# Folding the first block's closing norm into the next block's first norm, in a two-block network on one core

## The reference, cut to what matters

```
def rmsnorm(x, w): ...            # x / sqrt(mean(x*x) + 1e-6) * w

def first_block(x, ...):
    x = x + lru_mlstm_layer(rmsnorm(x, e_norm[0]), ...)
    x = x + ssd_layer(rmsnorm(x, o_norm[0]), ...)
    return rmsnorm(x, final_norm)

def second_block(x, norm1_g, w_in, ...):
    for l in range(2):
        h = rms_norm(x, norm1_g[l])
        q, k, v, gu, gv = jnp.split(h @ w_in[l], ...)
        ...
        x = x + mixed @ w_o[l]
        x = x + conv_gated_ffn(rms_norm(x, norm2_g[l]), ...)
    return x
```

## Time and profile before

| | |
|---|---|
| median of three runs | 3615.18 us |
| profiled execution | 3617.5 us |
| its span, first to last instruction | 3615.7 us |
| PE busy | 3509.0 us (97%) |
| DVE busy | 2717.7 us (75%) |
| ACT busy | 1893.6 us (52%) |
| POOL busy | 1648.0 us (46%) |
| mean granted PE clock | 0.989 |
| HBM read | 618.75 MB, 172 GB/s over the span |

### The profile page before, as it was taken

The page is one execution under the profiler, slowest core; times in us unless marked ns, Lnnn a source line. Parts: engine busy times, 40 slices in busy tenths (PEclk is TensorE's granted clock), DMA queues, the critical chain, the costliest instruction groups (busy, mean ns, idle before and its releaser), DMA issues.

```text
span 3615.7 us, 53014 instructions
## 1 busy us (share of the span) xinstructions
PE 3509.0 (97%) x19644; PEld 3020.8 (84%) x19644; DVE 2717.7 (75%) x4031; ACT 1893.6 (52%) x2865; POOL 1648.0 (46%) x1435
## 2 busy tenths in 40 slices
PE   8998999999999999998999999999998999999999
PEld 7887888888888788777888888888886888888888
DVE  8768886689899954676788758877676788758875
ACT  6555785455555544765444434444765444434443
POOL 4325672167787700143366405653143366306640
PEclk9999999999999999998999999999998999999999
DMA  5544556655555556433555665556543555665566
GB/s 193 169 152 137 167 180 187 188 181 180 165 169 176 167 162 182 151 128 111 181 187 187 184 189 187 187 181 192 177 133 109 185 187 187 186 189 187 187 184 178
DMA packets 177041, 624.38 MB, mean 173 GB/s; under 512 B 19784, under 2 KB 25616, under 8 KB 175760
## 3 DMA queue, kind: packets, MB, share of 16 engines
q1 hardware_dynamic: 171216, 606.11, 53.6%
q10 hardware_dynamic: 5568, 14.89, 1.1%
HBM read 618.75 MB, written 2.17 MB: 172 GB/s over the span
## 4 chain that ended last, share of the span: by engine, by line
PE 71%; DVE 10%; POOL 5%; ACT 3%; issue 3%; ACTq 0%; POOLq 0%; DVEq 0%
PE psG L517 42%; PE psG L515 23%; DVE WL L1274 3%; PE psG L514 2%; PE psM L540 1%; POOL SQ L1724 1%; ACT WH L763 1%; ACT L783 1%; DVE sdx L1287 1%; POOL SQ L1743 1%; POOL sdx L1726 1%; DVE Et L1527 1%; DVE Et L1534 0%; POOL GV L1864 0%; DVE Y L1279 0%
## 5 line engine op out<-in xcount | busy, mean ns | idle before, releaser
L517 PE MATMUL psG<-H,WH 128*128 128x512 f32 x5655 | 2028.4, 399 | 0.0
L1274 DVE TENSOR_TENSOR WL<-RAW,WH 128x1024 fp32r<-128x1024 f32 (+1 forms) x1162 | 1488.7, 1281 | 578.9 <-ACT WH L763 577.1
L763 ACT ACTIVATE WH<-RAW 128x1024 fp32r<-128x1024 f32 (+1 forms) x1162 | 1214.6, 1045 | 970.0 <-PE psG L517 956.3
L515 PE MATMUL psG<-H,WL 128*128 128x256 f32 x6032 | 1672.3, 287 | 0.3
L517 PEld LDWEIGHTS psG<-H,WH 128*128 128x128 f32 x5655 | 1072.4, 190 | 232.0
L515 PEld LDWEIGHTS psG<-H,WL 128*128 128x128 f32 x6032 | 1148.9, 190 | 46.1 <-issue 9.6
L517 PE MATMUL psG<-Y,WH 128*128 128x512 f32 x2816 | 999.7, 398 | 0.0
L515 PE MATMUL psG<-Y,WL 128*128 128x256 f32 x2944 | 811.6, 283 | 11.6 <-DVE Y L1281 10.6
L517 PEld LDWEIGHTS psG<-Y,WH 128*128 128x128 f32 x2816 | 531.7, 189 | 120.8
L515 PEld LDWEIGHTS psG<-Y,WL 128*128 128x128 f32 x2944 | 557.5, 189 | 26.5 <-DVE WL L1274 11.2
L1873 POOL TENSOR_SCALAR fou<-fsu,PAR 128x256 f32<-128x256 f32 x88 | 177.4, 2016 | 565.2 <-DVE fsu L1316 565.2
(11 more groups left out here) (344 smaller groups left out, 3601.5 us busy)
## 6 DMA issues: line engine op xcount, KB each, us to landing
RAW<-in_w_up SPq DMA_DIRECT2D x352, 512.0 KB, 3.7
RAW<-in_w_o_in SPq DMA_DIRECT2D x162, 512.0 KB, 3.7
RAW<-in_w_e_in SPq DMA_DIRECT2D x128, 512.0 KB, 3.6
RAW<-in_w_down SPq DMA_DIRECT2D x128, 512.0 KB, 3.5
RAW<-in_w_in SPq DMA_DIRECT2D x112, 512.0 KB, 3.6
RAW<-in_w_o SPq DMA_DIRECT2D x72, 512.0 KB, 3.6
RAW<-in_w_e_out SPq DMA_DIRECT2D x64, 512.0 KB, 4.5
RAW<-in_w_o_out SPq DMA_DIRECT2D x64, 512.0 KB, 3.7
```

What stands on the lines that cost most here:

```text
L515: ins = e.matmul(o[:, 0:T], wl, x[:, 0:T], start=False, stop=False, skip_group_check=True)
L517: ins = e.matmul(o, wh, x, start=False, stop=last)
L763: copy = lambda o, i, scale=1.0: e.activation(o, i, ACT.Copy, scale=scale)
L1274: tt(WL_[c % NRAW][:, 0:n], RAW_[c % NRAW][:, 0:n], WH_[c % NW][:, 0:n].bitcast(F32), SUB).then_inc(sem("wl"), 1)
```

## The change

Stage 1 becomes an ordinary folded norm with one thing more. The products `fnorm` times `norm1` are made once and kept in `halves`; the halves of H are made tile by tile from X times that product. Beside `ss`, POOL keeps a second sum, `s2`, of the squares of X times `fnorm`, which ACT computes (into two buffers instead of four, `fsq`). Behind the stage PE does two column sums, ACT makes `fr` from the first, DVE multiplies the second by `fr` twice, ACT makes a second root, and DVE multiplies the two factors to `rstd`. The writes of X (times `fnorm` and `fr`), which the residual stream needs later, follow one a beat from the twelfth beat on.

```
--- before.py
+++ after.py
@@ -381,9 +381,8 @@
     dts, dtv, dto, dtz = slots("dt", 4, 28)
 
 
-    f2 = [slots("f2d", 8, 21), slots("f2p", 8, 29)]
-    fsq = slots("fsq", 4, 37)
-    fr = slots("fr", 1, 41)[0]
+    fsq = slots("fsq", 2, 42)
+    s2, fr, ft = slots("fin", 3, 20)
 
 
     GV = [place(f"GV{i}", T, at=oY + (32 + i) * KB)[0][:, :] for i in range(8)]
@@ -437,8 +436,16 @@
     small = Banks(psM, [sem(f"bank{i}") for i in range(4)])
     qk_n = lambda kind, i: i // 2 * 10 + i % 2 if kind == "K" else i // 8 * 10 + 2 + i % 8
 
-    NORM_LAYER = {0: 1, 2: 3, 4: 4, 5: 5}
+    NORM_LAYER = {0: 1, 1: 2, 2: 3, 4: 4, 5: 5}
     GAIN = {0: ("pa", "o_norm"), 2: ("pc0", "norm2"), 4: ("pc0", "nextn"), 5: ("pc1", "norm2")}
+
+    def gain(stage, n):
+
+        if stage == 1:
+            return halves[:, 48 + n:49 + n], sem("gn5"), 1
+        key, name = GAIN[stage]
+        return par(key, name, n), sem(key), 16
+
     py_done = {}
     sum_done = {}
     out_of = lambda kind, i: psG[S.index[(kind, i)] % NG][:, 0:T]
@@ -616,18 +623,9 @@
                 if n == 15 and stage in NORM_LAYER:
                     w.wait_ge(sem("ssq"), sum(1 for s in NORM_LAYER if s <= stage) * 16)
                     colsum(("ss", NORM_LAYER[stage]), ss)
-            for off, last in ((3, False), (1, True)):
-                for r in at("res", b - off):
-                    if r // 16 == 1 and (r == 31) == last:
-                        n = r % 16
-                        w.wait_ge(sem("fsq"), n + 1)
-                        sums("fin", n, fsq[n % 4], 16)
-            for k in range(8):
-                for r in at("res", b - 2 - k):
-                    if r == 31:
-                        for i in (2 * k, 2 * k + 1):
-                            w.wait_ge(sem(f"f2sq{i % 2}"), i // 2 + 1)
-                            sums("fin2", i, f2[i % 2][i // 2], 16)
+                    if stage == 1:
+                        w.wait_ge(sem("ssq2"), 15)
+                        colsum("s2", s2)
 
         def ssd(b):
             for _ in at("dt", b - 8):
@@ -1032,36 +1030,30 @@
             for r in at("res", b - 2):
                 stage, n = divmod(r, 16)
                 if stage in NORM_LAYER:
-                    key, name = GAIN[stage]
+                    g, key, v = gain(stage, n)
                     w.wait_ge(sem("res"), r + 1)
-                    w.wait_ge(sem(key), 16)
-                    high(NORM_LAYER[stage], n, par(key, name, n))
+                    w.wait_ge(key, v)
+                    high(NORM_LAYER[stage], n, g)
+                    if stage == 1:
+
+                        if n >= 2:
+                            w.wait_ge(sem("ssq2"), max(n - 2, 1))
+                        e.activation(fsq[n % 2], X[n], ACT.Square, scale=par("pb", "fnorm", n)).then_inc(sem("fsq"), 1)
             for r in at("res", b - 5):
                 stage, n = divmod(r, 16)
                 if n == 15 and stage in NORM_LAYER:
                     layer = NORM_LAYER[stage]
-                    w.wait_ge(sem("ev"), evn[last_in[layer - 1]])
-                    root(small[("ss", layer)], rstd, 1.0 / D, sem("rstd"))
-            for off, last in ((2, False), (1, True)):
-                for r in at("res", b - off):
-                    if r // 16 == 1 and (r == 31) == last:
-                        n = r % 16
-                        w.wait_ge(sem("res"), r + 1)
-                        if n >= 4:
-                            w.wait_ge(sem("small"), sum_done[("fin", n - 4)])
-                        e.activation(fsq[n % 4], X[n], ACT.Square).then_inc(sem("fsq"), 1)
-            for r in at("res", b - 1):
+                    if stage == 1:
+                        root(small[("ss", layer)], fr, 1.0 / D, sem("fin_rms"))
+                    else:
+                        w.wait_ge(sem("ev"), evn[last_in[layer - 1]])
+                        root(small[("ss", layer)], rstd, 1.0 / D, sem("rstd"))
+            for r in at("res", b - 7):
                 if r == 31:
-                    root(small["fin"], fr, 1.0 / D, sem("fin_rms"))
-                    for n in range(16):
-                        w.wait_ge(sem("fin_x"), n + 1)
-                        high(2, n, par("pb", "norm1", n))
-                        if n % 2 == 0:
-                            e.activation(f2[0][n // 2], X[n], ACT.Square).then_inc(sem("f2sq0"), 1)
-            for r in at("res", b - 10):
-                if r == 31:
-                    w.wait_ge(sem("ev"), evn[last_in[1]])
-                    root(small["fin2"], rstd, 1.0 / D, sem("rstd"))
+                    w.wait_ge(sem("fin_s2"), 1)
+                    own.up(e.activation(rl, ft, ACT.Ln, bias=eps_c, scale=1.0 / D))
+                    w.wait_ge(own.sem, own.n)
+                    e.activation(ft, rl, ACT.Exp, scale=-0.5).then_inc(sem("fin_r2"), 1)
 
         def ssd(b):
             q = slice(0, 64)
@@ -1141,7 +1133,7 @@
             for l in range(2):
                 for i in at("K", b - 1):
                     if i == 2 * l:
-                        w.wait_ge(sem("small"), small["fin2"].done)
+                        w.wait_ge(sem("small"), small["s2"].done)
                         w.wait_ge(sem("f_lo"), 44 * l) if l else None
                         e.dma_start(CC, I["c_att"]).then_inc(sem("cc"), 16)
                         e.dma_start(WS, I["w_s"][l]).then_inc(sem("ws"), 16)
@@ -1464,20 +1456,28 @@
             for r in at("res", b - 3):
                 stage, n = divmod(r, 16)
                 if stage in NORM_LAYER:
-                    key, name = GAIN[stage]
-                    w.wait_ge(sem(key), 16)
+                    g, key, v = gain(stage, n)
+                    w.wait_ge(key, v)
                     w.wait_ge(sem("hh"), NORM_LAYER[stage] * 16 + n + 1)
-                    low(HL[n], X[n], HH[n], par(key, name, n), sem("hl"))
-            for r in at("res", b - 1):
+                    low(HL[n], X[n], HH[n], g, sem("hl"))
+            for r in at("res", b - 6):
                 if r == 31:
+
+                    use = small["s2"]
                     w.wait_ge(sem("fin_rms"), 1)
-                    for n in range(18):
-                        if n < 16:
-                            w.wait_ge(sem("res"), 17 + n)
-                            stt(X[n], X[n], par("pb", "fnorm", n), fr, MUL, MUL).then_inc(sem("fin_x"), 1)
-                        if n > 1:
-                            w.wait_ge(sem("hh"), 32 + n - 1)
-                            low(HL[n - 2], X[n - 2], HH[n - 2], par("pb", "norm1", n - 2), sem("hl"))
+                    tt(ft, use.ap[:, 0:T], fr, MUL).then_inc(use.sem, 1)
+                    w.wait_ge(use.sem, use.out)
+                    tt(ft, ft, fr, MUL).then_inc(sem("fin_s2"), 1)
+            for r in at("res", b - 8):
+                if r == 31:
+                    w.wait_ge(sem("fin_r2"), 1)
+                    tt(rstd, fr, ft, MUL).then_inc(sem("rstd"), 1)
+            for n in range(16):
+                for r in at("res", b - 12 - n):
+                    if r == 31:
+                        w.wait_ge(sem("hh"), 48)
+                        w.wait_ge(sem("ssq"), 32)
+                        stt(X[n], X[n], par("pb", "fnorm", n), fr, MUL, MUL).then_inc(sem("fin_x"), 1)
 
         def ssd(b):
             q = slice(0, 64)
@@ -1492,7 +1492,8 @@
                 w.wait_ge(own.sem, own.n)
                 e.tensor_tensor_scan(z, o, v, 0.0, MUL, ADD).then_inc(sem("dt_rows"), 1)
                 w.wait_ge(sem("pb"), 16)
-                ts(gn5[:, 0:64], par("pb", "dskip", 0, 64), 0.5, None, MUL).then_inc(sem("gn5"), 1)
+                own.up(ts(gn5[:, 0:64], par("pb", "dskip", 0, 64), 0.5, None, MUL))
+                tt(halves[:, 48:64], par("pb", "fnorm", 0, 16), par("pb", "norm1", 0, 16), MUL).then_inc(sem("gn5"), 1)
             for kind, off, o in (("sB", 10, sd_b), ("sC", 12, sd_c)):
                 for g in at(kind, b - off):
                     w.wait_ge(sem("odd_tanh"), 4 * g + (kind == "sC") + 1)
@@ -1779,7 +1780,7 @@
                     w.wait_ge(sem("res"), r + 1)
                     if n == 0:
 
-                        w.wait_ge(sem("small"), small[("ss", (1, 3, 4)[k - 1])].done) if k else None
+                        w.wait_ge(sem("small"), small[("ss", k)].done) if k else None
                         step(tt(ss, X[n], X[n], MUL), "ssq")
                     else:
                         sq_free()
@@ -1787,11 +1788,12 @@
                         w.wait_ge(own.sem, own.n)
                         w.wait_ge(sem("ssq"), k * 16 + n)
                         step(tt(ss, ss, sq, ADD), "ssq")
-            for r in at("res", b - 1):
-                if r == 31:
-                    for n in range(1, 16, 2):
-                        w.wait_ge(sem("fin_x"), n + 1)
-                        tt(f2[1][n // 2], X[n], X[n], MUL).then_inc(sem("f2sq1"), 1)
+                    if stage == 1:
+
+                        w.wait_ge(sem("fsq"), n + 1)
```

(5 more changed lines are left out.)

## The result

| | before | changed |
|---|---|---|
| median (4 runs each) | 3615.10 us | 3593.12 us (3591.03 to 3593.66) |
| profiled execution, its span | 3617.5, 3615.7 us | 3593.6, 3591.7 us |
| mean granted PE clock | 0.989 | 0.991 |

What follows compares the result with a forecast made beforehand. PE was taken as the limit inside the second output projection, with the closing norm on the path behind it. -6.9 - 17.5 + 0.4 + 0.7 = -23.3: 3594.2 us profiled, 3591.9 as a median, range 3588 to 3600.

Steps and rivals of the forecast that it cites:

- Conversion: Whole kernel: sum against the profiled 3617.5 us, then take 2.3 off for the median; within 7.2 us is no change.
- Part 1: Second output projection: fifteen column sums leave PE as POOL adds the squares, -6.9 us, with -6.4 as the other end.
- Part 2: Junction behind that projection: idle 6.5, sums 6.9, low clock and H pacing 4.1 all go, -17.5 us.
- Part 4: Work added on other engines (halves, Squares, X writes, second root): hidden by idle and cover, taken at 0.
- Part 3: Behind the projection on PE: one more column sum, over s2, +0.4 us, and a wait for POOL's last add, +0.7.
- The other bound: POOL's second add at the projection's end takes 0.80 us, leaving PE no wait for the sum over s2.
- The hand-off rival: At the junction POOL's last add stands behind a split and the second root runs late: +5.9 us, 3597.8; chance 0.12.
- The cover of 2.3 us: After the junction, the eighth weight chunk's split is ready about 2558.5, PE needs it at 2560.8: no wait.
- The junction alone: Rival: the projection keeps its pace and only the junction gains, 3591.9 + 6.9 = 3598.8 us; chance 0.08.
- Exposed writes: Rival: behind the junction each write of X holds a head chain, +7.7 us, 3599.6; chance 0.09.
- slower: Rival: in the projection ACT waits each tile for POOL's adds, 4.0 a tile, 64 us if wholly exposed, 3656; chance 0.03.

Runs made afterwards that it cites:

- the part undone: The changed kernel with the in-projection column sums of squares put back on PE, junction as changed: 3600.05 us, ratio to before 0.9960.
- a run that took away more than them: The kernel before without the second norm's squares and sixteen column sums, its second root replaced by a copy: 3609.23 us, ratio 0.9983.
- the four versions above: Changed kernel with side-by-side roots (3592.84 us); the same, X writes last in their beat (3592.87); changed, constants' loads early (3592.16); side-by-side roots, loads early (3592.34).

## Why the prediction was right, and where it was off

- **Conversion.** Forecast 3594.2 profiled, measured 3593.6. On the medians the total agrees within 1.2 us (3591.9, 3593.12), which is about the spread of runs; the gain was 22.0 of 23.3 forecast. The 2.3 us taken off for the median came to 0.5 in the changed kernel, whose profiled execution lay near its median while that of the kernel before lay high; so part of the agreement is luck, and the terms are the better test.
- **Part 1**, -6.9 (or -6.4): measured 7.09 in the trace, 6.9 in the time with the part undone (its runs lay 7 apart). The whole-stage comparison with the first projection was the better of the two ends; fifteen sums at 0.43 alone give 6.4, too little. Why a sum costs 0.47 there and not 0.43 no run says.
- **Part 2**, -17.5 with 6.5 idle, 6.9 sums, 4.1 clock and pacing: the whole is borne out, its split is not. From the last matmul to Q head 0's sum the stretch fell by 55.50 - 39.33 = 16.17, against -17.5 + 0.4 + 0.7 = -16.4 forecast. But two misses cancel in this: the wait of 0.7 for the second sum did not come, and one of 0.84 (part 4) did. The idle of 6.5 is gone. The sums' 6.9 is supported only by the 6.0 of a run that took away more than them. The low clock was shorter than the forecast had it: 0.68 is a mean to 1470, and the clock stood at 0.50 up to 1466 only, so the 4.1 left over holds more of other pacing than it says.
- **Part 3**, +0.4 and +0.7: the column sum cost 0.43; the wait for it was 0. The mis-sized term is the second add, taken at 1.61 us by the first projection's row; it took 0.92, since it starts behind DVE's split, with only 0.32 us left of DVE's next instruction. The other bound (0.80, no wait) was right. The hand-off rival had half a point, since the first add is the one that is held. The Trainium skill, SBUF — State Buffer, section Who interferes with whom, states that a DVE instruction with two SBUF inputs contends with a GpSimd instruction that reads SBUF, and that the port pair they share is an exclusive lock. The trace agrees, in size too: 1.61, 1.34, 0.92 and 0.80 us with 1.00, 0.74, 0.32 and 0.20 us left of the DVE instruction. The forecast read the square of the earlier trace rows in this way, but took the add's two durations as bounds without asking what each had begun beside.
- **Part 4**, 0: measured 0.84 us. The term taken at 0 failed, in where I looked. The cover of 2.3 us was reckoned for a chunk of weights, and no wait for WL came. PE waited instead for K head 0's square, which stands on ACT behind the second root and three transfer issues, and which I had not counted in that line. Either of them taken away ends this wait and opens another further on (0.65 or 1.03). The writes of X cost little, if anything, as they are placed: no run leaves them out, and the one that moved each behind the head's product was disturbed by a late load. All at once they cost 4.4 us of junction, so the bound was real.
- **Rivals.** "The junction alone" is excluded by the part undone. "Exposed writes" and "slower" show nowhere: after its first four tiles POOL has 7 to 8 us of idle between tiles (7.92 in the row at 1447.14), and PE's only wait inside the projection is the one of 1.0 us for Y that it had.
- **What cancelled.** By the traces the lead over before was 22.9 us at Q head 0's sum and 24.1 at the next projection. The other 1.2 us fell behind two waits of PE in the gating (5.1 and 3.8 us in both kernels), where the same matmuls run at half clock for a longer or shorter time. Before, and then changed, behind the first of them:

```profile
1652.00:1654.00 2.00, 0.55 (x1) 0.50 (x2) 2.00 (x6) 1.23 (x4) 0.00 (x0) 0.50 0.00 0
1654.00:1656.00 2.00, 2.00 (x7) 1.60 (x6) 1.97 (x4) 0.83 (x3) 1.42 (x1) 0.50 0.00 0
1656.00:1658.00 2.00, 2.00 (x9) 1.74 (x8) 2.00 (x4) 0.04 (x1) 1.34 (x3) 0.63 0.00 0
```

```profile
1629.00:1631.00 2.00, 0.45 (x1) 0.45 (x2) 2.00 (x7) 1.13 (x4) 0.00 (x0) 0.77 0.00 0
1631.00:1633.00 2.00, 2.00 (x6) 1.62 (x6) 1.97 (x4) 0.93 (x3) 1.32 (x1) 0.50 0.00 0
1633.00:1635.00 2.00, 2.00 (x12) 1.72 (x10) 2.00 (x4) 0.42 (x1) 1.45 (x3) 0.88 0.00 0
```

Nothing of the change lies there, and the changed kernel profiled again took 212.1 us over this stretch, as before (212.2), so the 1.2 us are not its gain. Why the clock came back sooner in one execution is not settled. Here it moves a total by 1 us, and what lies ahead of the second projection by up to 3.4 (its first addition lies between 1300.27 and 1303.68 in the versions run); the four versions above are within that.

## What to carry to other kernels

When a kernel already does the same thing well in another place, that place is the best estimate: the distance between the same two points at both junctions gave the gain within 1 us (within 0.3 only because two misses cancelled). Where PE is full, a small matmul off its list is worth its whole length, and adding squares on an engine that is idle beside it cost nothing here. An added link on an in-order engine is to be followed to every instruction queued behind it, transfer issues among them; and shortening it may only move the wait to the next link. Where totals wander by 2 or 3 us, compare distances between the same two points of the traces.

## What the runs showed of the hardware

- A POOL addition (128x256 float32, two inputs) begun inside a DVE instruction with two inputs in SBUF took 0.60 us and what was left of that instruction: 1.60 with 1.00 left, 1.34 with 0.74, 0.92 with 0.32, 0.80 with 0.20. Inside a DVE addition with one input in PSUM it took 0.73. Which of two accumulators it wrote made no difference.
- A load of a weight chunk took 3.5 to 4.2 us ahead of the constants' transfers in the changed kernel, and 7.4 to 9.6 us, over six traces, as the next load behind them. That the constants hold it is inferred from the order.
- Behind a wait of PE of 2.7 us (writes at once) the granted clock was 0.50 for at least 2 us; behind waits of 0.8 it stayed at 1.00. The level of 0.50 is 1.2 GHz, 1.00 is 2.4 GHz.
- Three transfer issues on ACT took 1.65 us of its list, half of a root.
